# One gate's projection beside a softmax attention: eight jobs of 256 columns instead of four of 512

## The reference, cut to what matters

```
h = layer_norm(x) * (1 + sc1) + sh1
z, xbc, dt_raw, q, k, v, f_raw, g_ssd, g_att = split(h @ w_in)
y_ssd = gated_rms_norm(ssd(...), z) @ w_ssd_o
o     = forgetting_attention(q, k, v, log_sigmoid(f_raw))   # 8 heads of 64, causal
y_att = o @ w_att_o
merged = sigmoid(g_ssd) * y_ssd + sigmoid(g_att) * y_att
```

## Time and profile before

| what | us |
|---|---|
| median of three runs (lowest, highest) | 2125.88 (2124.75, 2131.48) |
| the profiled execution, its own time | 2127.87 |
| its span in the trace | 2126.1 |
| PE busy in it, by the model of the profile | 1608.8 |
| attention with the fills, from its first score record to the end of its last value record | 269.18 to 334.60 |

### The profile page before, as it was taken

The page is one execution under the profiler, slowest core; times in us unless marked ns, Lnnn a source line. Parts: engine busy times, 40 slices in busy tenths (PEclk is TensorE's granted clock), DMA queues, the critical chain, the costliest instruction groups (busy, mean ns, idle before and its releaser), DMA issues.

```text
span 2126.1 us, 19636 instructions
## 1 busy us (share of the span) xinstructions
PE 1608.8 (76%) x8021; PEld 826.0 (39%) x8021; DVE 419.5 (20%) x912; ACT 284.0 (13%) x632; POOL 60.2 (3%) x79
## 2 busy tenths in 40 slices
PE   7999999799998999999999644555455446544544
PEld 3674654344443676777644311211131112211111
DVE  5521642422213122121325200000000000000001
ACT  6211222110001222222133100000000000000000
POOL 2000000000000100111100000000000000000000
PEclk9999999889999999999999776777687777877778
DMA  9999232849998642445427599999999999999996
GB/s 353 353 374 348 90 101 80 346 188 418 426 427 306 248 158 80 137 141 178 141 91 309 210 428 428 428 428 428 428 428 427 428 427 428 427 428 427 428 428 269
DMA packets 104236, 670.53 MB, mean 315 GB/s; under 512 B 8227, under 2 KB 10984, under 8 KB 71120
## 3 DMA queue, kind: packets, MB, share of 16 engines
q1 hardware_dynamic: 100000, 657.63, 75.9%
q0 software_dynamic: 3712, 11.11, 1.6%
q10 hardware_dynamic: 432, 0.49, 0.1%
HBM read 661.86 MB, written 7.34 MB: 315 GB/s over the span
## 4 chain that ended last, share of the span: by engine, by line
PE 62%; DMA 32%; DVE 2%; ACT 2%; SPq 1%; issue 1%; DVEq 0%; ACTq 0%
PE psum L1098 14%; PE psum L1087 12%; DMA ring<-in_w_up 11%; DMA ring<-in_w_down 11%; PE psum L1698 11%; DMA ring<-in_w_gate 9%; PE psum L1433 5%; PE psum L1465 3%; PE psum L1349 2%; PE psum L1400 2%; PE psum L1053 2%; PE psum L1179 1%; PE psum L1472 1%; SPq L785 1%; PE psum L1557 1%
## 5 line engine op out<-in xcount | busy, mean ns | idle before, releaser
L1698 PE MATMUL psum<-work,prob 128*32 128x512 f32 x1024 | 294.2, 739 | 162.2 <-DMA ring<-in_w_up 85.0
L1698 PE MATMUL psum<-ring,prob 128*32 128x512 f32 x1024 | 294.3, 739 | 140.9 <-DMA work<-in_w_up 82.5
L1098 PE MATMUL psum<-ring,hT 128*128 128x512 f32 x672 | 302.6, 596 | 5.0 <-ACT hT L181 4.2
L1087 PE MATMUL psum<-hT,ring 128*128 128x256 f32 x1152 | 270.4, 381 | 3.7 <-DMA ring<-in_w_in 1.7
L1087 PEld LDWEIGHTS psum<-hT,ring 128*128 128x128 f32 x1152 | 210.5, 190 | 37.3 <-issue 6.8
L1698 PE MATMUL psum<-work,hT 128*32 128x512 f32 x512 | 140.6, 711 | 83.8 <-DMA ring<-in_w_down 83.8
L1698 PE MATMUL psum<-ring,hT 128*32 128x512 f32 x512 | 140.6, 711 | 54.0 <-DMA work<-in_w_down 52.4
L1098 PEld LDWEIGHTS psum<-ring,hT 128*128 128x128 f32 x672 | 123.1, 192 | 137.1 <-issue 131.1
L1698 PEld LDWEIGHTS psum<-work,prob 128*32 128x32 f32 x1024 | 71.3, 132 | 268.5 <-issue 268.5
L1698 PEld LDWEIGHTS psum<-ring,prob 128*32 128x32 f32 x1024 | 71.4, 132 | 247.8 <-issue 246.8
L181 ACT ACTIVATE work<-psum 128x512 f32<-128x512 f32 (+2 forms) x99 | 57.1, 577 | 643.0 <-PE psum L1712 315.7
(11 more groups left out here) (334 smaller groups left out, 1424.4 us busy)
## 6 DMA issues: line engine op xcount, KB each, us to landing
work<-in_w_up SPq DMA_DIRECT2D x40, 2048.0 KB, 20.1
ring<-in_w_up SPq DMA_DIRECT2D x40, 2048.0 KB, 20.2
ring<-in_w_gate SPq DMA_DIRECT2D x38, 2048.0 KB, 19.2
work<-in_w_gate SPq DMA_DIRECT2D x38, 2048.0 KB, 19.6
work<-in_w_down SPq DMA_DIRECT2D x38, 2048.0 KB, 20.2
ring<-in_w_in SPq DMA_DIRECT2D x72, 1024.0 KB, 7.3
ring<-in_w_down SPq DMA_DIRECT2D x34, 2048.0 KB, 21.2
ring<-in_w_mod SPq DMA_DIRECT2D x24, 1024.0 KB, 13.3
```

Of the source, the lines that this page charges most:

```text
L1087: mm = pe.matmul(o[:, wide(j * S, S)], w[:, ch], actT[:, c, :], start=(c == 0), stop=(c == KC - 1))
L1098: mm = pe.matmul(o, lhs, w, start=(c == 0), stop=(c == KC - 1))
L1698: mm = pe.matmul(o[wide(i * CAP2, CAP2), :], lhs(chunks_per * piece + c, i), R.slot(l + i, (chunks_per, width))[:, c, wide(b * BANK, BANK) ...
```

## The change

`ga` is cut into quarters: for each of its two chunks of 512 columns four jobs, each of one token class and 256 of the 512 columns (`divmod(quarter, 2)` gives class and half). There are eight fills for the 16 iterations, so each has two iterations of its own, i = 0-1, 2-3, up to 14-15. A fill still has eight matmuls, now of 256 columns. The weights of one chunk are read by four jobs instead of two, and the slot is free after the fourth. ACT makes eight copies of 128x256 instead of four of 128x512. All later jobs have numbers higher by four, so their banks turn by four.

```diff
+        def quarter_fills(name, w, col0, n):
+            return [("chunk", name, i, quarter, w, col0) for i in range(n) for quarter in range(4)]
...
-                    load_chunk(f"{nm}_{c}", w, wide(col0 + c * BANK, BANK), job(nm, 2 * c + 1))
+                    load_chunk(f"{nm}_{c}", w, wide(col0 + c * BANK, BANK), first_job[f"{nm}_{c}_3"] if nm == "ga" else job(nm, 2 * c + 1))
...
-        ga_fills = chunk_fills("ga", w_in, GA0, 2)
-        fox_fills = ga_fills
+        fox_fills = quarter_fills("ga", w_in, GA0, 2)
...
-                    lhs = class_columns(actT[:, c, :], t) if name in ("gs", "ga") else actT[:, c, wide(t * P, P)]
+                    lhs = class_columns(actT[:, c, :], t) if name == "gs" else actT[:, c, wide(t * P, P)]
...
+            def quarter_job(name, i, quarter):
+
+                k = first_job[f"{name}_{i}_{quarter}"]
+                t, part = divmod(quarter, 2)
+                o = claim(k)
+                for c, w in pieces(f"{name}_{i}") if quarter == 0 else chunks(f"{name}_{i}"):
+                    mm = pe.matmul(o[:, 0:S], class_columns(hT[:, c, :], t), w[:, wide(part * S, S)], start=(c == 0), stop=(c == KC - 1))
+                    if c < KC - 1:
+                        yield
+                finish(k, mm)
...
-                return token_job(name, i, half, hT), KC
+                return quarter_job(name, i, half) if name == "ga" else token_job(name, i, half, hT), KC
...
+            def take_quarter(i, quarter):
+                t, part = divmod(quarter, 2)
+                take(first_job[f"ga_{i}_{quarter}"], sig_ga[:, t, wide(i * BANK + part * S, S)], src=lambda o: o[:, 0:S])
...
-                      [(lambda: None) if fill[0] == "unit" else (lambda fill=fill: take_gate("ga", 2 * fill[2] + fill[3], sig_ga)) for fill in fox_fills])
+                      [(lambda: None) if fill[0] == "unit" else (lambda fill=fill: take_quarter(fill[2], fill[3])) for fill in fox_fills])
```

## The result

The changed kernel takes 2117.80 us in the median of seven runs (2116.61 to 2119.32), the kernel before 2129.72 in seven (2124.70 to 2132.07). The ratio is 0.995, with a 95% interval of 0.9939 to 0.9961: between 8 and 13 us faster. The prediction was 2118 us. The kernel before scatters by 7 us, and the median of its seven runs lies 3.8 us above the 2125.88 of the three that I worked with. That the time was met within 0.2 us is luck in part: the baseline and the gain were both too low, and the two errors offset each other.

The account below looks back on a forecast made before the run. The prediction saw 62% of the span on PE, 32% on DMA. Gains of 5.3 + 1.7 + 1.9 = 8.9 us, taken from 2127.87 and 2125.88, gave 2119.0 and 2117.0; it took 2118 us, range for 8 in 10 2111 to 2126.

Parts of the forecast that it names:

- PE pauses where no fill stands: Attention: PE pauses only in stretches without a fill, in iterations 4, 7, 11 and behind the last scores, 5.6 us.
- The price of the columns: Fills: records of 256 columns take 0.219 us against 0.430 for 512, weight loads hidden, costing 0.5 us in all.
- The estimate of 1.5 times the cost for halves: Fills: by the skill's figures 13.6 us more, a loss of some 5 us; the prediction rejected it for fp32.
- The loss case with exposed loads: Rival, fills: strided weight loads not hidden under 256 columns, up to 24.3 us added, 2141 us; chance 0.05.
- The breaks: Attention pairs: exposed loads where fill records follow small ones, kept inside 3.55 us of small work for each pair.
- The end of the attention: From the values of tile 13 at full clock: 3.93 us instead of 5.66, a gain of 1.7 us.
- the first term: Attention up to the last scores: 54.5 us instead of 59.76, a gain of 5.3 us.
- The merging product: First merging product behind the attention: 6.87 us at full clock instead of 8.77, a gain of 1.9 us.
- The three together: Gains up to the last scores, at the attention's end and in the first merging product: 5.3 + 1.7 + 1.9 = 8.9 us.
- It reaches the end: Later stages: loads go out earlier by as much, so the gain of 8.9 us is carried whole.
- The loads: Slots of `ga` come free in iterations 7 and 15; att_o and w_o loads go at about 297 and 325; nothing waits.
- The clock: Attention and first merging product: half-clock falls vanish; rival that they stay loses 1.7 + 0.7 + 1.9 us, 2122 us; chance 0.20.

Follow-up runs that it names:

- the two gaps left open: The changed kernel with iterations 6-7 and 10-11 without a fill, their two jobs moved into iterations 4-5 and 8-9: 2120.58 us, ratio 0.9964 to the kernel before.

## Why the prediction was right, step by step

*PE pauses where no fill stands.* Right for iterations 7 and 11 and the end. The chain through DVE, ACT and the fill's copy that the earlier trace rows show is unchanged in the narrow jobs in old places and in the two gaps left open, where it makes pauses of 1.0 us (0.2 less than before by the narrower copy, as worked out). The pause of 0.78 us in iteration 4 was misread: a fill stands there, and it is the fill that waits.

```profile
282.52 0.39 ACT L181 ACTIVATE probT<-psum 128x256 f32<-128x256 f32 x1
...
282.95 1.13 PE L1098 MATMUL psum<-ring,hT 128*128 128x512 f32 x2 [0.79 <-ACT probT L181]
```

By the numbering this fill's bank is that of tile 1's transposed probabilities, and PE stands until ACT has copied them. The pause went because the fill's number, and with it its bank, changed, and not because work was put there; it is gone with the narrow jobs in old places too. In the same way "a fill's bank is that of the values job before it by eight" is wrong for the fills of iterations 2-3, where it is a score job, and 6-7 and 10-11, where it is a yT job. Those two made waits of 0.7 us each for the wide jobs moved there and are only just met in the changed kernel.

*The price of the columns.* Right in kind and size: records 0.22 us apart. The estimate of 1.5 times the cost for halves, worked out from two figures of the Trainium skill ("TensorE: Matmul & The Clock Gate", section "Back-to-back issue gap"), didn't come true for fp32. The loss case with exposed loads is excluded: 197 ns of load against 219 from record to record, with little to spare (the 213 ns that I set against the load stand in no row; half of a wide record's 430 is 215).

*The breaks.* Mis-sized, to the good. I carried 3.55 us of small work and breaks a pair; measured is 6.82 - 3.50 = 3.3. In the chain of iterations 8 and 9 before, the fill's records take 7.22 us, 0.35 more than the 6.87 of such a job alone; those of a pair after take 3.62, 0.12 more than 3.50. The break behind a small record is shorter with the narrow jobs, and I had carried over the one of the wide jobs. Over the eight pairs this is most of why the stretch to the last scores is 53.1 us where I had 54.5.

*The end of the attention.* 4.41 us where I had 3.93. I had the values of four records at 0.39; behind a wait they take 0.63 (two of those, 0.48 in all). The extra copy on ACT cost nothing. The gain of this term was 1.3 instead of 1.7. What I called 2.15 us of fill under the wait was 1.75 us of fill, a transpose pair and values; PE has 2.31 us of work there now and no pause. The whole attention, 57.50 us, lies just below the 58 to 59 that I named as the sign of being right: I had 1.4 us too much in the first term and 0.5 too little in this one.

*The merging product.* 6.92 where I had 6.87.

The three together: the attention and the merging product took 74.19 us and take 64.42, 9.8 us less against 8.9 predicted. The two errors, 1.4 and 0.5 us, have opposite signs, so the sum is closer than its terms.

*It reaches the end.* Right: the lead is 10.39 us at the second merging product and 10.19 at the latent projection (688 us), so the later stages gave back 0.2. *The loads* behind the slots of `ga` went out at 295.98 and 323.87 (I had about 297 and 325); nothing waited for them.

*The clock.* I gave the falls in the attention and the merging product 1.7 + 0.7 + 1.9 = 4.3 us and a chance of 0.20 to stay. The experiment with work in the pauses measures them at 4.3 us in the traces; with PE busy there is none. The Trainium skill ("TensorE: Matmul & The Clock Gate", section "HAM oscillation — how this bites in real kernels") lays such falls to longer idle gaps than the 1.2 us here. In these traces falls follow pauses of 1.2 and even 1.0 us, and filling the pauses took the falls away, so the measurement decides. Of the eight traces of kernels that still pause by 1.0 us or more, six have a fall (the three of before, two of the three of narrow jobs in old places, and the wide moved one) and two have none; of the four others none has one. So a pause of that length makes a fall possible and not certain. With four traces, and three of them of one kernel and its variants, this shows that the covered kernels fall less often, and not that they never do. The times of the kernel with products in the pauses (eight runs, 3 to 7 us below the kernel before) say the same.

How the 9.8 us divide, by attentions at full clock: 4.3 us are the clock. Of the rest, 62.99 - 57.50 = 5.5 us, the narrow jobs alone give 2.0 (62.99 to 61.01: the wait of 0.8 us in iteration 4 gone, because the fill's bank is now another job's; two copies 0.2 us shorter; about 0.5 in the fills of iterations 4-5, 8-9 and 12-13, which take 7.06 us each in the chain against 7.2 to 7.3; 0.3 at the end, whose cause stays open). Fills in iterations 2-3 and 12 to 15 give another 1.1 (61.01 to 59.88: PE's idle time falls from 4.3 to 2.6 us, and its busy time rises by 0.5), and the two yT pauses 2.4 (59.88 to 57.50).

What stays open: the kernel before scattered over 8 us and more from run to run, and only three of its executions have a trace. The clock at the places seen here (low for 17 us against 10 around the attention, 14 to 24 around 420) goes some way towards that; I can't say that it is all.

## What to carry to other kernels

Independent work beside a chain of small dependent steps pays by where it stands: cut it so fine that every step of the chain has some, as long as the smaller pieces still cover their weight loads (here 197 ns of load, 219 from record to record). When a wait of PE is weighed, add what the clock may take behind it: here 4.3 us beside pauses of 5.6. And whenever jobs are added or moved under a rotating bank assignment, look which job's bank each of them now inherits: here that took one wait of 0.8 us away and, for the wide jobs moved to other places, made two of 0.7 and one of 1.0.

## What the runs showed that I hadn't expected

Products that nobody reads, put into PE's pauses, made the kernel before 5.4 us faster in the median (2122.60 against 2128.01) and the changed one 3.3 us faster up to the first expert product. Behind pauses of 1.0 and 1.2 us the granted clock was 0.50 for 3.4 to 6.8 us in some executions and not in others, for the same kernel. And four value records that take 0.39 us in the flow take 0.63 behind a wait at full clock.
